# Moving a transpose, a masked product and a scaling between engines in the chunked delta-rule scan

## The chip, the cores and the metric

The kernel runs on one core of one Trainium2 chip. The metric is the device time of one execution in microseconds (us); the same program is executed several times and the median is reported. Engine names below are those of the profile: PE is TensorE (PEld its weight loads), DVE is VectorE, ACT is ScalarE, POOL is GpSimd, SP is SyncE, which issues the DMAs.

## The reference, cut to what matters

The model has two parts: a block with a gated delta-rule mixer and a feed-forward layer, and then two layers of a second network. The change lies in the delta-rule mixer alone. It works on chunks of 64 tokens, 8 heads, two directions, over 256 context tokens and 512 latent ones:

```
kk = k k^T                                   # per chunk, 64 x 64
a_mat = where(strict, beta * kk * decay, 0) + I
rhs = [v * beta, k * (beta * exp(gc))]
sol = triangular_solve(a_mat, rhs)           # unit lower triangle
u, w = sol[..., :dv], sol[..., dv:]
step:  v_new = u - w s
       o = (q * exp(gc)) s + (q k^T * decay) v_new
       s = s * exp(g_last) + k_dec^T v_new
```

All is float32.

## The kernel before

**The stages.** The program is written out per engine, in order, with semaphores between the engines; each engine executes its own list strictly in order. Two *scans*, one for each group of 4 heads (`hg` 0 and 1), stand between long projection stages. The functions `pe_scan`, `act_scan`, `dve_scan` and `pool_scan` hold the four engines' lists of a scan.

**Units and phases.** A scan has 12 units, `s` from 0 to 11. A unit is one chunk in each direction for 4 heads, with the two directions on the two halves of the 128 partitions. Units 0 to 3 are context, units 4 to 11 are latent. Each unit has five tiles of 128x512, shown as `u` in the profile: XY (X in columns 0 to 255, Y in 256 to 511), BA (A and, behind it, its transpose AT), EP, EQ and R. Tiles are shared by units that are 4 apart, which is why a unit's first phase waits until unit `s - 4` is done (`slot_free`).

The phases of a unit are

- `ga`: POOL makes the masked log decays in X.
- `kk`: PE multiplies k by k and sums the decays; ACT takes the exponential; POOL multiplies by beta; DVE makes A.
- `qk` (latent only): the decays for q and the product q k.
- `tr`: PE transposes A by 8 matmuls with the identity (`at`) and ACT copies the result into AT; POOL makes X = A * mask of level 0 (`x0`); DVE adds the identity to X (the *tr add*).
- `pt` (latent only): the transpose of the q k product.
- `ax` and `xy`, levels 1 to 5: the inverse of the triangular matrix is doubled level by level. `ax`: PE multiplies AT and X, DVE masks the product into E (the *level mask*). `xy`: PE multiplies E with X and Y, DVE adds both to XY. In `ax` of level 1 PE also makes Y as the transpose of X (`y0`, 8 matmuls with the identity) and ACT copies it into Y. In `ax` of levels 1 to 4, ACT makes one head of R = V * beta per level, in two halves (`bv`).
- `ks`: k times the state, and DVE adds it into R. `vn`: Y times R, the new values. `out`: PE makes the state's increment and the output; DVE updates the state tile `ss` with 8 instructions (the *state update*), then adds or ACT copies the output.

**The order.** `gdn_order()` interleaves the units in turns: in one turn each live unit has one phase, the oldest unit first. A unit joins every four or five turns, so that three or four are live. The same order holds on all four engines. In a turn with a `tr`, the unit in `tr` is the newest, and so its instructions stand last in the turn on each engine; the next instruction on DVE is then the first of the next turn, of an older unit. For latent units the turns around `tr` are

```
turn 36   5:vn   6:xy4  7:xy2  8:tr
turn 37   5:out  6:ax5  7:ax3  8:pt
turn 38   6:xy5  7:xy3  8:ax1  9:ga
...
turn 45   7:out  8:xy4  9:ax2  10:tr
turn 46   8:ax5  9:xy2  10:pt  11:ga
turn 47   8:xy5  9:ax3  10:ax1 11:kk
```

So on DVE the tr add is followed by the state update of the oldest unit (after units 4, 7, 8 and 11), or by an add or a level mask for PE (after 5, 6, 9 and 10). The context units have turns such as

```
turn 10   0:xy4  1:xy2  2:tr
turn 11   0:ax5  1:ax3  2:ax1
turn 12   0:xy5  1:xy3  2:xy1  3:ga
```

POOL's own list around these is `0tr 1ga 1kk 1tr 2ga 2kk 2tr 3ga 3kk 3tr 4ga 4kk 4qk 4tr 5ga ...`.

**PSUM.** All PE results go to a ring of 8 banks (`ps`), taken in order. Helper lines: L205 is any matmul, L224 any ACT activation, L236 a DVE or POOL tensor-tensor operation, L244 a DVE operation with a scalar and a tensor.

A matmul of float32 shows as two instructions in the trace, so that 8 matmuls are x16.

Of the kernel before, what the change touches and what calls it, by code (L numbers as in the profile page):

```python
# [66 lines left out]
def level_table():  # L67


    r, c = np.arange(128)[:, None], np.arange(64)[None, :]  # L70

    def mask(b, par):
        low = ((r % 64) // (2 * b) == c // (2 * b))
        low, up = low & ((r // b) % 2 == 1) & ((c // b) % 2 == 0), low & ((r // b) % 2 == 0) & ((c // b) % 2 == 1)
        return np.where(np.where((par + r // 64) % 2 == 0, low, up), -1.0, 0.0)

    out = [mask(b, par) for b in (1, 2, 4, 8, 16, 32) for par in range(2)]
    return np.concatenate(out, 1).astype(np.float32)


# [290 lines left out]
class Kernel:  # L371
# [56 lines left out]
    def layout(self):  # L428
# [32 lines left out]
        self.lbt = self.sb("lbt", m + 256, [128, 6, 16])  # L461
        self.sml = self.ring("sml", [self.sb("sml", m + 384 + 64 * i, [128, 64]) for i in range(8)])
        self.dec = self.ring("dec", [self.sb("dec", W + 33792 + 64 * i, [128, 64]) for i in range(4)])
        self.lvl = self.sb("lvl", B, [128, 12, 64])
        self.SS = self.sb("ss", B + 832, [128, 2, 512])
        self.bias = self.sb("bias", B, [128, 8, 384])

# [756 lines left out]
    def pe_scan(self, hg):  # L1224
# [6 lines left out]
        for s, ph in gdn_order():  # L1231
# [29 lines left out]
            elif ph == "pt":  # L1261
                b = K.ps.take(pe, "pt", *z)
                pe.wait_ge(dve.at("p", *z))
                for h in hs:
                    for r in rows:
                        pe.mm(Q(b, h)[r, :], Q(PP, h)[r, :], id_[r, r])
                pe.mark("pt", *z)
            elif ph[0] == "ax":
                lv = ph[1]
                b = K.ps.take(pe, "ax", *z, lv)  # L1270
                pe.wait_ge(act.at("at", *z), dve.at("xy", *z, lv - 1))
                for h in hs:
                    for r in rows:
                        pe.mm(Q(b, h)[r, :], Q(AT, h)[r, :], Q(X, h)[r, :])
                pe.mark("ax", *z, lv)
                if lv == 1:
                    b = K.ps.take(pe, "y0", *z)
                    for h in hs:
                        for r in rows:
                            pe.mm(Q(b, h)[r, :], Q(X, h)[r, :], id_[r, r])  # L1280
                    pe.mark("y0", *z)
            elif ph[0] == "xy":
                lv = ph[1]
                b = K.ps.take(pe, "xy", *z, lv)
                pe.wait_ge(dve.at("ev", *z, lv), act.at("y0", *z))
                for h in hs if lv < 5 else ():
                    for r in rows:
                        pe.mm(Q(b, h)[r, :], Q(Y, h)[r, :], Q(E, h)[r, :])
                for h in hs:
                    for r in rows:  # L1290
                        pe.mm(Q(b, 4 + h)[r, :], Q(E, h)[r, :], Q(Y, h)[r, :])
                pe.mark("xy", *z, lv)
            elif ph == "ks":
                b = K.ps.take(pe, "ks", *z)
                pe.wait_ge(dve.at("s", hg, s - 1))
                for h in hs:
                    for d, hf, c in pair:
                        pe.mm(H(b, h)[rows[hf], :], K.KT[:, h, tok[d]], H(K.SS[:, d, :], h))
                pe.mark("ks", *z)
            elif ph == "vn":  # L1300
                b = K.ps.take(pe, "vn", *z)
                pe.wait_ge(act.at("bv", *z) if s == 0 else dve.at("r", *z), dve.at("xy", *z, 5))
                for h in hs:
                    for r in rows:
                        pe.mm(H(b, h)[r, :], Q(Y, h)[r, :], H(R, h)[r, :])
                pe.mark("vn", *z)
                if lat:
                    b = [K.ps.take(pe, "o", *z, d) for d in range(2)]
                    pe.wait_ge(pool.at("q", *z))
                    for h in hs:  # L1310
                        for d, hf, c in pair:
                            pe.mm(Q(b[d], h), H(K.SS[:, d, :], h), EQ[:, h * 128 + hf * 64:h * 128 + hf * 64 + 64], h == 0, False,
                                  skip=True)
                    pe.mark("os", *z)
            elif ph == "out":
                if s < 11:
                    b = [K.ps.take(pe, "s", *z, d) for d in range(2)]
                    pe.wait_ge(dve.at("vd", *z))
                    for h in hs:
                        for d, hf, c in pair:  # L1320
# [17 lines left out]
    def act_scan(self, hg):  # L1338
# [3 lines left out]
        for s, ph in gdn_order():  # L1342
# [14 lines left out]
            elif ph == "pt":  # L1357
                act.wait_ge(pe.at("pt", *z))
                act.cp(EP[:, 256:512], K.ps[("pt", *z)][:, 0:256]).then_inc(act("pt", *z), 1)
                act.also("ps", "pt", *z)  # L1360
            elif ph[0] == "ax":
                h = ph[1] - 1
                if h == 0:
                    act.wait_ge(pe.at("y0", *z))
                    act.cp(XY[:, 256:512], K.ps[("y0", *z)][:, 0:256]).then_inc(act("y0", *z), 1)
                    act.also("ps", "y0", *z)
                for d, hf, c in K.pair(s) if h < 4 else ():
                    r = slice(64 * hf, 64 * hf + 64)
                    v, o = K.VM[r, c // 2, h * 128:h * 128 + 128], R[r, h * 128:h * 128 + 128]
                    act.a(o, v, ACT.Copy, scale=K.col(K.beta, s, hg, h)[r]).then_inc(act("bv", *z), 1)  # L1370
            elif ph == "vn":
                act.wait_ge(pe.at("vn", *z), dve.at("vd", *z) if s < 11 else None)
                act.cp(BA, K.ps[("vn", *z)]).then_inc(act("vn", *z), 1)
# [11 lines left out]
    def dve_scan(self, hg):  # L1385
# [5 lines left out]
        for s, ph in gdn_order():  # L1391
# [9 lines left out]
                dve.tt(PP, K.ps[("qk", *z)][:, 0:256], E, ALU.mult).then_inc(dve("p", *z), 1)  # L1401
                dve.also("ps", "qk", *z)
            elif ph == "tr":
                X = XY[:, 0:256]
                dve.wait_ge(pool.at("x0", *z))
                dve.tt(q4(X), q4(X), bc4(K.con("id64")), ALU.add).then_inc(dve("xy", *z, 0), 1)
            elif ph[0] == "ax":
                lv = ph[1]
                dve.wait_ge(pe.at("ax", *z, lv), dve.at("p" if lat else "a", *z) if lv == 1 else pe.at("xy", *z, lv - 1))
                b, m = K.ps[("ax", *z, lv)][:, 0:256], K.lvl[:, lv * 2 + par, :]  # L1410
                dve.tt(q4(E), q4(b), bc4(m), ALU.mult).then_inc(dve("ev", *z, lv), 1)
                dve.also("ps", "ax", *z, lv)
            elif ph[0] == "xy":
                lv = ph[1]
                w = slice(0 if lv < 5 else 256, 512)
                dve.wait_ge(pe.at("xy", *z, lv), dve.at("xy", *z, lv - 1), act.at("y0", *z))
                dve.tt(XY[:, w], XY[:, w], K.ps[("xy", *z, lv)][:, w], ALU.add).then_inc(dve("xy", *z, lv), 1)
                dve.also("ps", "xy", *z, lv)
            elif ph == "ks":
                dve.wait_ge(pe.at("ks", *z), act.at("bv", *z))  # L1420
                b = K.ps[("ks", *z)]
                for h in hs:
                    dve.stt(H(R, h), H(b, h), K.col(K.nbe, s, hg, h), ALU.mult, H(R, h), ALU.add).then_inc(dve("r", *z), 1)
# [25 lines left out]
    def pool_scan(self, hg):  # L1449
        K, pool, pe, act, dve = self, self.pool, self.pe, self.act, self.dve  # L1450
        pool.wait_ge(K.ended("chunks", hg), dve.at("nbe"))
        q4 = lambda ap: ap.rearrange("p (a b) -> p a b", b=64)
        v4 = lambda ap: ap.rearrange("p (a b) -> p a b", b=128)
        for s, ph in gdn_order():
            par, lat, (XY, BA, EP, EQ, R) = K.unit(s)
            z = (hg, s)
            X, A, E = XY[:, 0:256], BA[:, 0:256], EP[:, 0:256]
            if ph == "ga":
                pool.wait_ge(K.slot_free(z))
                pool.tt(q4(X), bc4(K.con(f"strict{par}")), bcl(K.cols(K.gg, s, hg), 64), ALU.mult).then_inc(pool("ga", *z), 1)  # L1460
            elif ph == "kk":
                pool.wait_ge(act.at("ev", *z))
                pool.tt(q4(A), q4(E), bcl(K.cols(K.beta, s, hg), 64), ALU.mult).then_inc(pool("eb", *z), 1)
                if lat:
                    pool.wait_ge(pool.at("eb", *z))
                    pool.tt(q4(E), q4(E), bc4(K.con(f"keep{par}")), ALU.mult).then_inc(pool("evm", *z), 1)
            elif ph == "qk":
                for d, hf, c in K.pair(s):
                    v = v4(EQ)[:, :, hf * 64:hf * 64 + 64]
                    pool.wait_ge(act.at("eq", *z))  # L1470
                    pool.tt(v, v, K.QT[:, :, (c - 4) * 64:(c - 3) * 64], ALU.mult).then_inc(pool("q", *z), 1)
            elif ph == "tr":
                pool.wait_ge(dve.at("a", *z), pe.at("kk", *z))
                pool.tt(q4(X), q4(A), bc4(K.lvl[:, par, :]), ALU.mult).then_inc(pool("x0", *z), 1)
            elif ph == "out":
                pool.mark("unit", *z)
        pool.mark("end", "scan", hg)
# [1685 lines left out]
```

## Time and profile before

| what | value |
|---|---|
| median of 3 executions | 4074.79 us (4074.69 to 4075.39) |
| profiled execution, its own time | 4075.39 us |
| its span in the profile | 4073.2 us |
| PE busy | 3790.8 us (93%) |
| DVE busy | 1935.7 us (48%) |
| ACT busy | 1510.6 us (37%) |
| POOL busy | 770.0 us (19%) |
| mean granted PE clock | 0.957 |

The span runs from the first to the last instruction of the profiled execution; the execution's own time is 2.2 us longer. "Busy" is the time in which an engine executed something; weight loads overlap the matmuls. The two scans lie at about 295 to 500 us and 640 to 851 us of the span, about a tenth of it.

### The profile page before, as it was taken

The numbers are of one execution on the slowest core, as the hardware profiler recorded it, in microseconds if no ns is written. First come the engines' busy times: TensorE is split into PE (matmuls) and PEld (weight loads), VectorE is DVE, ScalarE is ACT, GpSimd is POOL, SyncE is SP. The second block draws the span as 40 slices with busy tenths as digits, with TensorE's granted clock in tenths as the row PEclk, the third lists the DMA queues.
The fourth block names the chain that finished last, engine by engine and source line by source line (L and its number), as shares of the span: only waits on it lengthen the run. The fifth ranks groups of instructions, "written<-read, shape, count | busy, mean of one in ns | idle before, by whom it ended". The sixth has DMA issues, their size and how long they took to land.

```text
span 4073.2 us, 60895 instructions
## 1 busy us (share of the span) xinstructions
PE 3790.8 (93%) x25654; PEld 3075.0 (75%) x25654; DVE 1935.7 (48%) x3078; ACT 1510.6 (37%) x2533; POOL 770.0 (19%) x790
## 2 busy tenths in 40 slices
PE   6889998999999999988999999998999799999998
PEld 3568887887888747776888788875677688777886
DVE  5556555535444565635334533336465533444333
ACT  3433233323323345734223332224575422343222
POOL 0122122221211123432111110102244211101010
PEclk8999999989999899999999999998999899999999
DMA  5321010012222202111223122220111022222222
GB/s 183 125 84 18 3 52 13 3 53 104 99 96 96 68 16 72 59 58 37 97 95 119 59 97 99 97 79 26 62 63 63 16 96 96 88 102 84 98 94 87
DMA packets 81111, 300.87 MB, mean 74 GB/s; under 512 B 8776, under 2 KB 9928, under 8 KB 79944
## 3 DMA queue, kind: packets, MB, share of 16 engines
q1 hardware_dynamic: 80840, 296.99, 21.5%
q8 instruction: 203, 3.33, 0.3%
q14 instruction: 68, 0.56, 0.0%
HBM read 292.76 MB, written 4.19 MB: 73 GB/s over the span
## 4 chain that ended last, share of the span: by engine, by line
PE 75%; DVE 10%; ACT 6%; issue 5%; POOL 3%; DMA 1%; DVEq 0%; SPq 0%; POOLq 0%; ACTq 0%
PE ps L205 74%; PE ps L210 1%; DVE wlo L236 1%; DVE he L244 1%; ACT whi L224 1%; DVE hc L2334 1%; DVE tmp L244 1%; ACT ha L224 1%; DVE ac L244 1%; ACT wp L225 1%; DVE ha L236 1%; ACT L224 1%; DVE ss L244 1%; DVE q L236 1%; DMA wraw<-weights 0%
## 5 line engine op out<-in xcount | busy, mean ns | idle before, releaser
L236 DVE TENSOR_TENSOR wlo<-wraw,whi 128x1024 fp32r<-128x1024 f32 x537 | 682.1, 1275 | 771.6 <-ACT whi L224 770.9
L205 PE MATMUL ps<-hh,whi 128*128 128x512 f32 x1840 | 733.4, 399 | 19.1 <-DVE hl L236 13.9
L205 PE MATMUL ps<-hl,whi 128*128 128x512 f32 x1840 | 723.8, 393 | 0.0
L205 PE MATMUL ps<-hh,wlo 128*128 128x512 f32 x1840 | 723.5, 393 | 0.0
L224 ACT ACTIVATE whi<-wraw 128x1024 fp32r<-128x1024 f32 x537 | 559.8, 1050 | 223.1 <-PE ps L205 169.6
L205 PEld LDWEIGHTS ps<-hh,whi 128*128 128x128 f32 x1840 | 349.8, 190 | 103.7 <-ACT hh L224 20.1
L205 PEld LDWEIGHTS ps<-hh,wlo 128*128 128x128 f32 x1840 | 350.1, 190 | 74.7
L205 PEld LDWEIGHTS ps<-hl,whi 128*128 128x128 f32 x1840 | 350.7, 191 | 70.7
L205 PE MATMUL ps<-u,u 64*64 64x64 f32 (+2 forms) x6016 | 229.0, 228 | 25.6 <-DVE u L236 17.0
L205 PEld LDWEIGHTS ps<-u,u 64*64 64x64 f32 (+1 forms) x6016 | 209.5, 139 | 42.3 <-DVE u L236 18.1
L205 PE MATMUL ps<-gh,whi 128*128 128x512 f32 x528 | 205.4, 389 | 0.0
L205 PE MATMUL ps<-gl,whi 128*128 128x512 f32 x528 | 205.4, 389 | 0.0
L205 PE MATMUL ps<-gh,wlo 128*128 128x512 f32 x528 | 205.4, 389 | 0.0
L236 POOL TENSOR_TENSOR gl<-fv,gh 128x512 fp32r<-128x512 f32 x66 | 85.3, 1293 | 593.8 <-ACT gh L224 593.8
L236 POOL TENSOR_TENSOR sml<-sml,con 128x4 f32<-128x4 f32 (+3 forms) x36 | 60.5, 1681 | 665.7 <-DVE sml L241 603.6
L224 ACT ACTIVATE u<-ps 128x256 f32<-128x256 f32 (+1 forms) x128 | 57.7, 451 | 255.3 <-PE ps L205 189.4
L205 PE MATMUL ps<-fh,whi 128*128 128x512 f32 x352 | 138.5, 393 | 3.5 <-DVE fl L244 2.6
L205 PE MATMUL ps<-fl,whi 128*128 128x512 f32 x352 | 137.7, 391 | 0.0
L205 PE MATMUL ps<-fh,wlo 128*128 128x512 f32 x352 | 137.7, 391 | 0.0
L224 ACT ACTIVATE gh<-fv 128x512 fp32r<-128x512 f32 x66 | 41.7, 632 | 250.1 <-DVE fv L236 250.1
L236 DVE TENSOR_TENSOR x<-x,ps 128x512 f32<-128x512 f32 x64 | 44.0, 688 | 189.7 <-PE ps L205 189.7
L224 ACT ACTIVATE accs<-x 128x512 f32<-128x512 f32 x56 | 35.4, 632 | 243.6 <-DVE x L236 185.8
(391 smaller groups left out, 7145.7 us busy)
## 6 DMA issues: line engine op xcount, KB each, us to landing
wraw<-weights SPq DMA_DIRECT2D x537, 512.0 KB, 3.2
x<-xT SPq DMA_DIRECT2D x2, 2048.0 KB, 12.4
bias_lines<-ln SPq DMA_DIRECT2D x1, 2048.0 KB
xmf<-memT SPq DMA_DIRECT2D x2, 1024.0 KB, 4.7
out<-x SPq DMA_DIRECT2D x1, 2048.0 KB, 6.2
bias<-bias_lines SPq DMA_DIRECT2D x1, 1536.0 KB, 8.7
con<-consts SPq DMA_DIRECT2D x1, 1378.0 KB, 10.5
ctxt<-ctxT SPq DMA_DIRECT2D x1, 1024.0 KB, 12.5
```

The costliest lines, as they stand in the source:

```text
L205: self.last, self.open = self.e.matmul(out, lhsT, rhs, start=start, stop=stop, skip_group_check=skip), True
L210: self.last, self.open = self.e.transpose(out, in_, idn[0:k, 0:k]), True
L224: return self.e.activation(out, in_, func, bias=bias, scale=scale)
L225: return self.e.activation(out, in_, func, bias=bias, scale=scale, accum_out=acc)
L236: return self.e.tensor_tensor(out, a, b, op)
L244: return self.e.scalar_tensor_tensor(out=out, in0=a, scalar=s, in1=b, op0=op0, op1=op1)
L2334: dve.e.tensor_tensor_scan(C[:, r], rst[:, r], A[:, r], 0.0, ALU.mult, ALU.add).then_inc(dve("hb", *z), 1)
```

## The change

Four edits, all in the scan:

1. `y0` is gone: PE no longer transposes X, ACT no longer copies Y. Instead POOL's product in `tr` covers both halves of XY: X = A * mask and Y = AT * mask of the other direction. Its masks lie beside each other in the table `lvl`, which has 13 rows instead of 12. It now waits for ACT's copy of AT, beside the wait for A.
2. DVE's tr add covers 512 columns instead of 256.
3. `bv` moves from ACT (8 instructions of 64x128 per unit) to POOL (2 instructions of 64x512 per unit), in `ax` of level 2. POOL waits for its own last instruction before each, and for the end of each before it goes on (`halved`).
4. The consumers wait for the new producers: `vn` of unit 0 and `ks` wait for POOL's `bv`; `xy` no longer waits for `y0`.

```diff
@@ level_table
-    out = [mask(b, par) for b in (1, 2, 4, 8, 16, 32) for par in range(2)]
+    out = [mask(1, 0), mask(1, 1), mask(1, 0)] + [mask(b, par) for b in (2, 4, 8, 16, 32) for par in range(2)]
@@ pe_scan
                 pe.mark("ax", *z, lv)
-                if lv == 1:
-                    b = K.ps.take(pe, "y0", *z)
-                    for h in hs:
-                        for r in rows:
-                            pe.mm(Q(b, h)[r, :], Q(X, h)[r, :], id_[r, r])
-                    pe.mark("y0", *z)
...
-                pe.wait_ge(dve.at("ev", *z, lv), act.at("y0", *z))
+                pe.wait_ge(dve.at("ev", *z, lv))
...
-                pe.wait_ge(act.at("bv", *z) if s == 0 else dve.at("r", *z), dve.at("xy", *z, 5))
+                pe.wait_ge(pool.at("bv", *z) if s == 0 else dve.at("r", *z), dve.at("xy", *z, 5))
@@ act_scan
-            elif ph[0] == "ax":
-                h = ph[1] - 1
-                if h == 0:
-                    act.wait_ge(pe.at("y0", *z))
-                    act.cp(XY[:, 256:512], K.ps[("y0", *z)][:, 0:256]).then_inc(act("y0", *z), 1)
-                    act.also("ps", "y0", *z)
-                for d, hf, c in K.pair(s) if h < 4 else ():
-                    r = slice(64 * hf, 64 * hf + 64)
-                    v, o = K.VM[r, c // 2, h * 128:h * 128 + 128], R[r, h * 128:h * 128 + 128]
-                    act.a(o, v, ACT.Copy, scale=K.col(K.beta, s, hg, h)[r]).then_inc(act("bv", *z), 1)
@@ dve_scan
             elif ph == "tr":
-                X = XY[:, 0:256]
-                dve.wait_ge(pool.at("x0", *z))
-                dve.tt(q4(X), q4(X), bc4(K.con("id64")), ALU.add).then_inc(dve("xy", *z, 0), 1)
+                dve.wait_ge(pool.at("xy0", *z))
+                dve.tt(q4(XY), q4(XY), bc4(K.con("id64"), 8), ALU.add).then_inc(dve("xy", *z, 0), 1)
@@ pool_scan
             elif ph == "tr":
-                pool.wait_ge(dve.at("a", *z), pe.at("kk", *z))
-                pool.tt(q4(X), q4(A), bc4(K.lvl[:, par, :]), ALU.mult).then_inc(pool("x0", *z), 1)
+                pool.wait_ge(dve.at("a", *z), act.at("at", *z), pe.at("kk", *z))
+                m = K.lvl[:, par:par + 2, :].unsqueeze(2).broadcast_to([128, 2, 4, 64])
+                t = lambda ap: ap.rearrange("p (a h b) -> p a h b", a=2, h=4)
+                pool.tt(t(XY), t(BA), m, ALU.mult).then_inc(pool("xy0", *z), 1)
+                last = pool.at("xy0", *z)
+            elif ph == ("ax", 2):
+                for d, hf, c in K.pair(s):
+                    r = slice(64 * hf, 64 * hf + 64)
+                    pool.wait_ge(halved, pool.at("xy0", *z), K.slot_free(z), last)
+                    pool.tt(v4(R)[r], v4(K.VM[r, c // 2, :]), bcl(K.cols(K.beta, s, hg)[r], 128), ALU.mult).then_inc(pool("bv", *z, hf), 1)
+                    halved = pool.at("bv", *z, hf)
+                pool.also("bv", *z)
```

## Rows read from the trace of the kernel before

**Rows 1.** Busy time by engine in the two scans; columns as printed.

```profile
core 0: us, PE busy (x) PEld busy (x) DVE busy (x) ACT busy (x) POOL busy (x), PEclk, DMA share, GB/s
295.00:500.00 205.00, 188.47 (x4362) 172.22 (x4362) 116.55 (x295) 67.91 (x168) 39.29 (x60) 0.97 0.10 13
645.00:851.00 206.00, 192.64 (x4390) 176.83 (x4386) 116.11 (x294) 66.84 (x167) 37.84 (x58) 0.96 0.01 3
```

**Rows 2.** The chain that ended last, in order of time: start us, us, what.

```profile
377.41 0.04 issue
377.45 34.77 PE ps L205 x804
```

**Rows 3.** Who waited for whom, first scan: us in total, times, longest us.

```profile
DVE u L236 <- POOL u L236: 33.5, 14, 10.0
```

**Rows 4.** Groups of instructions, first scan: count, busy us, mean ns, idle before.

```profile
L224 ACT ACTIVATE u<-vm,beta 64x128 f32<-64x128 f32 x96 | 37.0, 396 | 1.8
L236 DVE TENSOR_TENSOR u<-u,ps 128x512 f32<-128x512 f32 x48 | 32.6, 686 | 21.3 <-PE ps L205 21.0
...
L205 PEld LDWEIGHTS ps<-con,u 64*64 64x64 f32 x512 | 18.5, 140 | 4.6 <-DVE u L236 4.6
...
L236 POOL TENSOR_TENSOR u<-u,lvl 128x256 f32<-128x256 f32 x12 | 8.7, 724 | 2.3 <-DVE u L236 2.3
```

**Rows 5.** Groups of POOL instructions, start of the span to 860 us.

```profile
L236 POOL TENSOR_TENSOR kt<-ac,sg 128x512 f32<-128x512 f32 x8 | 10.3, 1288 | 0.0
```

**Rows 6.** Timeline around `tr` of unit 8: start us, us, engine, instruction, idle before.

```profile
410.42 0.55 PEld L205 LDWEIGHTS ps<-con,u 64*64 64x64 f32 x16
...
411.16 0.39 ACT L224 ACTIVATE u<-ps 128x256 f32<-128x256 f32 x1 [3.02 <-PE ps L205]
411.30 0.42 DVE L236 TENSOR_TENSOR u<-u,con 128x256 f32<-128x256 f32 x1
...
412.25 2.16 DVE L244 SCALAR_TENSOR_TENSOR ss<-ss,ex,ps 128x128 f32<-128x128 f32 x8 [0.54 <-PE ps L205]
...
414.79 1.94 PEld L205 LDWEIGHTS ps<-u,u 64*64 64x64 f32 x64 [0.26 <-DVE u L236]
```

**Rows 7.** Timeline around `tr` of unit 2.

```profile
319.98 0.55 PEld L205 LDWEIGHTS ps<-con,u 64*64 64x64 f32 x16
...
320.52 0.61 POOL L236 TENSOR_TENSOR u<-con,gg 128x256 f32<-128x256 f32 x1
320.71 0.39 ACT L224 ACTIVATE u<-ps 128x256 f32<-128x256 f32 x1 [2.10 <-PE ps L205]
320.87 0.55 DVE L236 TENSOR_TENSOR u<-u,con 128x256 f32<-128x256 f32 x1
...
321.34 1.37 DVE L236 TENSOR_TENSOR u<-ps,lvl 128x256 f32<-128x256 f32 x3
...
322.46 4.25 PEld L205 LDWEIGHTS ps<-u,u 64*64 64x64 f32 x128
```

**Rows 8.** Timeline, the tr add of unit 0 beside a POOL instruction.

```profile
301.16 0.61 POOL L236 TENSOR_TENSOR u<-con,gg 128x256 f32<-128x256 f32 x1
301.24 0.82 DVE L236 TENSOR_TENSOR u<-u,con 128x256 f32<-128x256 f32 x1 [0.84 <-POOL u L236]
```

**Rows 9.** Timeline around `tr` of unit 10.

```profile
443.90 1.41 POOL L236 TENSOR_TENSOR u<-u,qt 128x256 f32<-128x256 f32 x2 [4.47 <-ACT u L224]
...
448.34 0.39 ACT L224 ACTIVATE u<-ps 128x256 f32<-128x256 f32 x1 [1.06 <-PE ps L205]
...
448.88 0.42 DVE L236 TENSOR_TENSOR u<-ps,lvl 128x256 f32<-128x256 f32 x1
...
450.01 1.55 PEld L205 LDWEIGHTS ps<-u,u 64*64 64x64 f32 x48
```

**Rows 10.** Timeline around `tr` of unit 6.

```profile
376.66 0.39 ACT L224 ACTIVATE u<-ps 128x256 f32<-128x256 f32 x1 [2.23 <-PE ps L205]
...
378.18 0.42 DVE L236 TENSOR_TENSOR u<-ps,lvl 128x256 f32<-128x256 f32 x1
...
379.31 1.55 PEld L205 LDWEIGHTS ps<-u,u 64*64 64x64 f32 x48
```

More of the change, by code:

```diff
@@ L463, in layout @@
         self.dec = self.ring("dec", [self.sb("dec", W + 33792 + 64 * i, [128, 64]) for i in range(4)])
-        self.lvl = self.sb("lvl", B, [128, 12, 64])
+        self.lvl = self.sb("lvl", B, [128, 13, 64])
         self.SS = self.sb("ss", B + 832, [128, 2, 512])
@@ L1409, in dve_scan @@
                 dve.wait_ge(pe.at("ax", *z, lv), dve.at("p" if lat else "a", *z) if lv == 1 else pe.at("xy", *z, lv - 1))
-                b, m = K.ps[("ax", *z, lv)][:, 0:256], K.lvl[:, lv * 2 + par, :]
+                b, m = K.ps[("ax", *z, lv)][:, 0:256], K.lvl[:, 1 + lv * 2 + par, :]
                 dve.tt(q4(E), q4(b), bc4(m), ALU.mult).then_inc(dve("ev", *z, lv), 1)
@@ L1415, in dve_scan @@
                 w = slice(0 if lv < 5 else 256, 512)
-                dve.wait_ge(pe.at("xy", *z, lv), dve.at("xy", *z, lv - 1), act.at("y0", *z))
+                dve.wait_ge(pe.at("xy", *z, lv), dve.at("xy", *z, lv - 1))
                 dve.tt(XY[:, w], XY[:, w], K.ps[("xy", *z, lv)][:, w], ALU.add).then_inc(dve("xy", *z, lv), 1)
@@ L1419, in dve_scan @@
             elif ph == "ks":
-                dve.wait_ge(pe.at("ks", *z), act.at("bv", *z))
+                dve.wait_ge(pe.at("ks", *z), pool.at("bv", *z))
                 b = K.ps[("ks", *z)]
@@ L1453, in pool_scan @@
         v4 = lambda ap: ap.rearrange("p (a b) -> p a b", b=128)
+        halved = None
         for s, ph in gdn_order():
@@ L1457, in pool_scan @@
             X, A, E = XY[:, 0:256], BA[:, 0:256], EP[:, 0:256]
+            pool.wait_ge(halved)
             if ph == "ga":
@@ L1460, in pool_scan @@
                 pool.tt(q4(X), bc4(K.con(f"strict{par}")), bcl(K.cols(K.gg, s, hg), 64), ALU.mult).then_inc(pool("ga", *z), 1)
+                last = pool.at("ga", *z)
             elif ph == "kk":
@@ L1463, in pool_scan @@
                 pool.tt(q4(A), q4(E), bcl(K.cols(K.beta, s, hg), 64), ALU.mult).then_inc(pool("eb", *z), 1)
+                last = pool.at("eb", *z)
                 if lat:
@@ L1466, in pool_scan @@
                     pool.tt(q4(E), q4(E), bc4(K.con(f"keep{par}")), ALU.mult).then_inc(pool("evm", *z), 1)
+                    last = pool.at("evm", *z)
             elif ph == "qk":
@@ L1471, in pool_scan @@
                     pool.tt(v, v, K.QT[:, :, (c - 4) * 64:(c - 3) * 64], ALU.mult).then_inc(pool("q", *z), 1)
+                    last = pool.at("q", *z)
             elif ph == "tr":
-                pool.wait_ge(dve.at("a", *z), pe.at("kk", *z))
-                pool.tt(q4(X), q4(A), bc4(K.lvl[:, par, :]), ALU.mult).then_inc(pool("x0", *z), 1)
+                pool.wait_ge(dve.at("a", *z), act.at("at", *z), pe.at("kk", *z))
[10 more added lines that the diff above has]
+                pool.also("bv", *z)
             elif ph == "out":
```

## The prediction

> **What bounds the kernel now.** I read the table of busy time by stretch first, because the change touches only the two scans, a tenth of the span. In the first scan PE is busy for 188.47 of 205.00 us, in the second for 192.64 of 206.00; DVE for 116, ACT for 67 and POOL for 38 to 39 [rows 1]. So PE is the bound of a scan and only some 13 to 17 us of idle PE time are left in each. The chain that ended last says the same in order of time: from 377.45 us it stays on PE for 34.77 us without a break [rows 2], and outside of such stretches it goes over DVE. Two consequences. Work taken from PE is worth its full length; work taken from ACT is worth nothing unless something waited for it. And DVE, busy for only 57%, does its work in order: PE waits as soon as one DVE instruction in its list is held up by more than the lead that PE has. What holds DVE up before is mostly POOL: 33.5 us in 14 waits [rows 3], which are the waits in `kk`, that the change leaves alone, and the start. The second scan has the same list on every engine; I work one out and take it twice.
>
> **The parts.**
>
> *PE without `y0`.* The `at`, `pt` and `y0` transposes are 32 blocks of 16 instructions in a scan; their weight loads, which set the pace, take 18.5 us for 512 [rows 4], so 0.58 us a block. 12 blocks go per scan: 12 x 0.58 = 7.0 us. This is the gain, 13.9 us in both scans if PE loses nothing in return.
>
> *ACT without the copy of Y and without `bv`.* 96 instructions of 396 ns and 12 of 0.39 [rows 4, 6] are 42 us of ACT per scan. But ACT waited for PE before each of the AT copies that I looked at (2.10, 2.23, 3.02 and 1.06 us idle) [rows 6, 7, 9, 10]. No queue stood in front of them, so nothing starts sooner. I count nothing. If the cover were gone, a copy behind one `bv` piece would be 0.4 us late; the idle times exclude that here.
>
> *The product on POOL: later and longer.* Before, it needs only A and is finished before DVE comes to the tr add. Now it needs AT, and so stands behind PE's `at` and ACT's copy. Its length goes from 724 ns at 256 columns [rows 4] to what 512 columns of the same operation take: 1288 ns [rows 5]. Bounds from rows: 0.72, if the second half were free, and 1.45, if it were twice the first. The row has the same width and type, so I take 1.29. A hand-over between engines costs 0.04 us, as in the chain [rows 2].
>
> *The tr add* goes from 0.42 [rows 6] to 0.69, as the other 128x512 adds [rows 4].
>
> These two lie on one path: `at`, AT copy, product, tr add, and behind the tr add everything that stands later in DVE's list. How much reaches PE differs by unit.
>
> *Units 4, 7, 8, 11 (state update next).* Unit 8: the copy ends at 411.16 + 0.39 = 411.55, the product runs from 411.59 to 412.88, the add from 412.92 to 413.61. The state update, which began at 412.25, begins 1.35 us later. Behind it stand the level masks for which PE was already idle at 414.79 (0.26 us) [rows 6]. There is no lead left, so all 1.35 us reach PE. Four units: 5.4 us.
>
> *Units 5, 6, 9, 10 (an add or a level mask next).* Unit 10: copy ends at 448.73, product until 450.06, add until 450.79. The level mask moves from 448.88 to 450.75 and ends at 451.2. PE wants its result in the block that began at 450.01 [rows 9], so PE waits for 1.2 us, and a little more for the add behind: 1.3. Unit 6: copy ends at 377.05, product until 378.38, add until 379.11, mask from 379.1 to 379.5 instead of from 378.18; PE wanted it at 379.31 [rows 10]: 0.2 to 0.3. By the same sum unit 5 is like 6 and unit 9 a little under 10. I take 0.3, 0.3, 1.0 and 1.3: 2.9 us. The ends are 0 and the full delay of the mask, 0.9 to 1.9 each.
>
> *Units 0 to 3 (context).* There is no turn between `tr` and `ax` of level 1, so PE also waits directly for X. Unit 2: the copy ends at 321.10, the product at 322.43. POOL then goes on at once to `ga` of the next unit, 0.61 us, and this meets the tr add. The trace has that meeting: the add, 0.42 us when alone, took 0.82 and ended 0.29 us after the POOL instruction (301.77, 302.06), and took 0.55 and ended again 0.29 after it (321.13, 321.42) [rows 7, 8]. So the new add, 0.27 longer, ends 0.56 after `ga`: 322.43 + 0.02 + 0.61 + 0.56 = 323.62, instead of 321.42. `ax` level 1 of unit 2 (at least 0.48, a third of the 48-instruction block) follows at 323.66, and the next block, which began at 322.46 after `y0`, begins near 324.15: 1.7 us later, with the gain of `y0` already in it. Units 0 and 1 stand in the same order (`0tr 1ga`, `1tr 2ga`): 1.7 each. Behind unit 3, POOL waits elsewhere and DVE was busier: 1.0. Sum: 6.1 us.
>
> The Trainium skill ("SBUF — State Buffer", section "Who interferes with whom") has this as a rule: a VectorE instruction with two SBUF inputs contends with a GpSimd instruction that reads SBUF, and the later one to issue blocks until the first ends. By the full wait of the rule the add of unit 0 would have ended 0.4 after POOL, by the row 0.29; that is 0.1 us in three units per scan.
>
> *`bv` on POOL.* No POOL instruction of the trace has 64 partitions. Bounds: 0.64 us, half of 128x512, and 1.29, the whole. I take 1.2, two per unit, so 29 us more of POOL per scan: 39 becomes about 75 of 205 us with the longer products. Where could it be late? Before the product of unit 10, the tightest place: q's two products end at 445.31, then `bv` of unit 9 until 447.8, and the product is not ready before 448.77 [rows 9]. There is room for 1.7 us a piece. What is queued behind it on POOL (`kk`, `qk` of the next unit) waits for ACT for longer than that. R is wanted only in `ks`, ten turns on. So `bv` costs nothing in the sum.
>
> The Trainium skill ("GPSIMD Engine Reference", section "2. Architecture") gives each of the 8 cores 16 fixed partitions. By that rule 64 partitions would take as long as 128, 1.29 us; no row here shows it, and the sum would be the same.
>
> *DMA, tables and banks.* The level table is one row longer, in one load at the start. The ring loses a bank user per unit, which can only free banks sooner.
>
> **The sum** per scan: 6.1 + 5.4 + 2.9 - 8 x 0.58 = 9.8 us. Two scans: 19.5 us. On the profiled execution's own 4075.4 us (span 4073.2) this is 4094.9; that execution was 0.6 over the median, so I say 4094.5.
>
> **The rivals.**
>
> *The stalls hide and `y0` decides (faster).* PE has a lead over DVE, the stalls eat only that, and 13.9 us remain as gain: 4061. It decides if PE's lead at the tr add is over 1.35 us in every latent unit and the context units cost no more than `y0`. Units 5 and 6 come near. Against it: the idle PE time before 414.79, and the context units, where PE itself needs X. Chance 0.10.
>
> *Only the context units show (no change).* The latent stalls are hidden but those of units 0 to 3 not: 2 x 6.1 - 2 x 8 x 0.58 = +2.9, so 4078; with half of the state-update stalls, +8.3, the border. Chance 0.15.
>
> *The tr add is also kept out by `bv` (slower still).* After units 0, 1 and 2 POOL's list has `ga` and then both `bv` pieces with nothing to wait for but POOL itself. If POOL takes up the next piece before the blocked add gets in, each of these 6 adds loses another 1.2 to 2.4 us: +7 to +14, so 4102 to 4109. For it: the add did get in only after the POOL instruction's end in rows 7 and 8. Against: POOL waits for its own completion in between, which leaves a gap. Chance 0.15. In the same direction, full exposure in the four mask units adds 2 x 3 = 6 us.
>
> The Trainium skill's rule of the exclusive lock, named above, is what would make this one bite.
>
> *The forecast*, a net loss of 12 to 27 us: 0.60.
>
> **How the numbers follow.** A measurement of this kernel tells 0.2%, 8 us, from no change. Slower by more: the forecast 0.60 and the lock rival 0.15: 0.75. Within 0.2%: 0.15. Faster: 0.10. The forecast's own range is 4087 to 4102. The low end of the range goes into the no-change case, 4080, the high end to the end of the lock rival with a product of 1.45 us, 4111. What is left out is the faster case and half of the no-change case.
>
> **What would show it.** In the profile after: POOL's product at about 1.29 us, beginning 0.04 to 0.1 after ACT's copy; in the list of waits, DVE waiting for POOL about 12 times more per scan and some 15 to 20 us more in total; PE waiting for DVE by about 15 us more; PE busy 7 us less per scan, and each scan 9 to 10 us longer. The state update after `tr` of unit 8 should begin more than 2 us after PE's `at` ends, and not 1.2. ACT should be near 25 us busy. If scans are longer but DVE's waits are not, my mechanism is wrong; if DVE waits and PE does not, PE's lead was larger than I read. The prediction fails if POOL needs much less than 1.29 us for 512 columns, or if the turn has slack that a single unit's rows don't show: a late DVE instruction that lets PE run on with the next phase, and catches up.

## The result and the profile after

| | time |
|---|---|
| before, 6 executions beside the changed kernel | 4079.11 us median (4074.69 to 4094.03) |
| changed kernel, 6 executions | 4113.70 us median (4109.05 to 4118.91) |
| ratio | 1.0082, 95% interval 1.0062 to 1.0100 |
| profiled execution of the changed kernel | 4119.53 us, span 4117.7 us |

The change makes the kernel slower by 33 us (25 to 41). The forecast was slower, but by 19.5 us, and its 4094.5 and its range (4080 to 4111) end below the measured median. About 4 us of the distance is the kernel before itself, whose first three executions, on which the forecast stood, were at its low end; the rest is the change.

I measure a scan from the start of the first A on DVE to the start of the last level mask. In the first profiles the second scan goes from 195.9 to 213.5 us, +17.6; +9.8 was forecast. Two windows that each run from about that first A to just behind the last mask split this into idle and busy time of PE. Columns as in [rows 1]; the kernel before:

```profile
644.00:842.00 198.00, 185.16 (x4338) 170.20 (x4340) 115.41 (x291) 66.24 (x166) 38.11 (x58) 0.98 0.01 3
```

and the changed kernel:

```profile
673.00:888.00 215.00, 186.62 (x4140) 170.24 (x4142) 120.31 (x291) 25.86 (x58) 70.82 (x82) 0.94 0.01 3
```

PE idles for 215.00 - 186.62 = 28.4 us instead of 12.8: +15.6. And it is busy for 1.5 us *more*, although 192 instructions (the 12 blocks of `y0`) are gone, which were worth 7.0 us. The granted clock over the window went from 0.98 to 0.94.

Around `tr` of unit 8, second scan, the changed kernel's timeline answers to [rows 6]:

```profile
797.10 0.55 PEld L205 LDWEIGHTS ps<-con,u 64*64 64x64 f32 x16
...
797.83 0.38 ACT L224 ACTIVATE u<-ps 128x256 f32<-128x256 f32 x1 [3.03 <-PE ps L205]
798.35 1.26 POOL L236 TENSOR_TENSOR u<-u,lvl 128x512 f32<-128x512 f32 x1 [4.25 <-DVE u L236]
...
799.64 0.69 DVE L236 TENSOR_TENSOR u<-u,con 128x512 f32<-128x512 f32 x1 [1.59 <-POOL u L236]
...
800.25 2.15 DVE L244 SCALAR_TENSOR_TENSOR ss<-ss,ex,ps 128x128 f32<-128x128 f32 x8
...
802.79 1.94 PEld L205 LDWEIGHTS ps<-u,u 64*64 64x64 f32 x64 [1.58 <-DVE u L236]
```

Read it downwards: transposes, copy, product, add, state update, and then PE, each waiting for the one above. The state update begins 3.15 us after the start of `at` instead of 1.83 [rows 6]: 1.32 late, 1.35 was forecast. PE's wait goes from 0.26 to 1.58 us. The waits of the second scan (us in total, times, longest) say the same, after:

```profile
DVE u L236 <- POOL u L236: 51.0, 24, 10.0
...
PE ps L205 <- DVE u L236: 27.4, 20, 3.2
```

and before:

```profile
DVE u L236 <- POOL u L236: 33.5, 14, 10.0
...
PE ps L205 <- DVE u L236: 12.2, 12, 3.2
```

DVE has ten more waits for POOL, 17.5 us in total, and PE waits 15.2 us more for DVE.

Stretches of 10 us at the start of the second scan show where the clock went. The changed kernel:

```profile
668.00:678.00 10.00, 3.73 (x43) 2.74 (x45) 1.51 (x2) 2.05 (x3) 3.98 (x5) 0.50 0.01 2
678.00:688.00 10.00, 8.40 (x143) 6.96 (x140) 2.55 (x5) 0.72 (x2) 1.93 (x3) 0.60 0.01 2
688.00:698.00 10.00, 7.25 (x210) 6.54 (x208) 4.81 (x9) 0.43 (x2) 4.78 (x5) 1.00 0.01 2
698.00:708.00 10.00, 7.99 (x196) 7.76 (x193) 5.72 (x12) 0.57 (x2) 4.17 (x4) 0.83 0.02 4
708.00:718.00 10.00, 8.10 (x199) 7.37 (x199) 5.79 (x12) 1.18 (x3) 2.45 (x3) 0.93 0.01 2
718.00:728.00 10.00, 10.00 (x215) 9.11 (x213) 5.17 (x12) 1.58 (x3) 4.73 (x6) 0.90 0.01 3
728.00:738.00 10.00, 7.63 (x168) 7.24 (x166) 5.77 (x16) 0.77 (x2) 1.88 (x2) 0.83 0.01 2
```

The kernel before, in its first profile:

```profile
640.00:650.00 10.00, 5.62 (x77) 4.47 (x75) 1.67 (x3) 3.52 (x7) 1.91 (x3) 0.50 0.00 0
650.00:660.00 10.00, 8.19 (x219) 7.30 (x217) 4.40 (x9) 3.76 (x11) 1.91 (x3) 0.97 0.01 3
660.00:670.00 10.00, 9.75 (x287) 9.14 (x286) 6.24 (x13) 3.40 (x10) 1.92 (x3) 1.00 0.02 4
```

and in another one, `before_again`:

```profile
655.00:665.00 10.00, 7.50 (x113) 6.76 (x114) 2.78 (x5) 2.25 (x6) 1.30 (x2) 0.50 0.01 2
665.00:675.00 10.00, 9.75 (x214) 8.31 (x215) 4.68 (x9) 4.13 (x11) 1.91 (x3) 0.81 0.01 3
675.00:685.00 10.00, 10.00 (x292) 9.53 (x294) 6.40 (x13) 4.04 (x11) 1.91 (x3) 1.00 0.02 4
```

All these scans begin at half clock (0.50, the level of 1.2 GHz); before them PE had little to do (2.29 us busy between 630 and 640 us in the first profile of the kernel before). When the clock comes up is no mark of the change: 6.4 us after the first A in the first profile of the kernel before, 13.7 and 14.0 in its two others, 13.1 and 13.2 in the two of the changed kernel. What the change brings is that the clock falls back behind waits. In the changed kernel's profile above it does so three times, for 10 us in all: the stretches at 0.83, at 0.93 and 0.90 (one fall across their border), and at 0.83. Each began within 1.5 us of the end of a wait of 1.9 to 2.4 us, those behind `tr` of units 2, 3 and 4. In its second profile, `after_again`, the same three waits were followed by one fall. In no second scan of the kernel before does the clock fall back. A block of 64 instructions that follows a wait of 2.37 us shows what such a fall means:

```profile
733.79 3.43 PEld L205 LDWEIGHTS ps<-u,u 64*64 64x64 f32 x64 [2.51 <-DVE u L236]
733.79 3.57 PE L205 MATMUL ps<-u,u 64*64 64x64 f32 x64 [2.37 <-DVE u L236]
```

Its weight loads take 3.43 us, where those of the same block at full clock take 1.94, before the change [rows 6] as behind `tr` of unit 8 after it. The Trainium skill ("TensorE: Matmul & The Clock Gate", "Part 1: The HAM clock gate") says that the clock has two levels and is set by how busy PE was of late. By that rule a wait can cost more than its own length, and this block agrees, with 1.5 us on top of its wait.

### The profile page after: what moved, and what is told of

It reads as the page before. It is cut to its first block, busy times and chain, and to the rows that moved or that the text cites. A ratio compares the mean times of both kernels' runs of the same rounds, so it can differ in the third digit from the quotient of the medians.

```text
span 4117.7 us, 59944 instructions
## 1 busy us (share of the span) xinstructions
PE 3797.1 (92%) x25270; PEld 3078.3 (75%) x25270; DVE 1945.4 (47%) x3078; ACT 1429.2 (35%) x2317; POOL 834.5 (20%) x838
## 4 chain that ended last, share of the span: by engine, by line
PE 64%; DVE 9%; ACT 5%; issue 3%; POOL 2%; DVEq 0%; POOLq 0%; ACTq 0%
PE ps L205 63%; DVE he L244 1%; PE ps L210 1%; DVE wlo L236 1%; DVE hc L2333 1%; ACT ha L224 1%; ACT wp L225 1%; DVE ha L236 1%; DVE tmp L244 1%; DVE q L236 1%; ACT whi L224 0%; ACT L224 0%; DVE ws L244 0%; POOL u L236 0%; DVE hl L236 0%
## 5 line engine op out<-in xcount | busy, mean ns | idle before, releaser
L205 PE MATMUL ps<-u,u 64*64 64x64 f32 (+2 forms) x6016 | 241.2, 236 | 62.5 <-DVE u L236 47.6
L205 PEld LDWEIGHTS ps<-u,u 64*64 64x64 f32 (+1 forms) x6016 | 220.8, 146 | 81.8 <-DVE u L236 33.2
L205 PE MATMUL ps<-gh,whi 128*128 128x512 f32 x528 | 205.4, 389 | 0.0
L205 PE MATMUL ps<-gl,whi 128*128 128x512 f32 x528 | 205.4, 389 | 0.0
L205 PE MATMUL ps<-gh,wlo 128*128 128x512 f32 x528 | 205.4, 389 | 0.0
L224 ACT ACTIVATE u<-ps 128x256 f32<-128x256 f32 (+1 forms) x104 | 48.4, 466 | 382.0 <-PE ps L205 289.1
L236 POOL TENSOR_TENSOR mg<-mg,mg 128x512 f32<-128x512 f32 x32 | 54.5, 1702 | 324.5 <-DVE mg L236 324.5
## 6 DMA issues: line engine op xcount, KB each, us to landing
ctxt<-ctxT SPq DMA_DIRECT2D x1, 1024.0 KB, 11.6
```

What stands on the lines that cost most here:

```text
L205: self.last, self.open = self.e.matmul(out, lhsT, rhs, start=start, stop=stop, skip_group_check=skip), True
L224: return self.e.activation(out, in_, func, bias=bias, scale=scale)
L236: return self.e.tensor_tensor(out, a, b, op)
```

## The experiments

Lengths of the scans in the profiles, from the first A to the last level mask, and the whole kernel by its ratio to the kernel before (us worked out with 4080):

| kernel | first scan | second scan | ratio (95% interval) | us |
|---|---|---|---|---|
| before (three profiles) | 195.8, 207.8, 208.4 | 195.9, 197.4, 197.4 | 1 | 0 |
| changed (two profiles) | 219.7, 219.5 | 213.5, 210.3 | 1.0082 (1.0062 to 1.0100) | +33 |
| `y0_only` | 218.5 | 213.6 | 1.0071 (1.0051 to 1.0092) | +29 |
| `bv_pool` | 196.8 | 196.8 | 0.9986 (0.9969 to 1.0003) | -6 |
| `wait_only` | 216.7 | 205.4 | 1.0039 (1.0025 to 1.0054) | +16 |
| `fill` | 224.5 | 207.2 | 1.0053 (1.0035 to 1.0070) | +22 |
| `fill_before` | 214.7 | 201.0 | 1.0022 (1.0006 to 1.0038) | +9 |
| `late_add` | 210.3 | 205.3 | 1.0008 (0.9994 to 1.0021) | +3 |
| `late_fill` | 213.8 | 197.9 | 0.9999 (0.9985 to 1.0013) | 0 |
| `split_ctx` | 213.2 | 204.3 | 1.0023 (1.0009 to 1.0037) | +9 |
| `split` (two profiles) | 191.7, 205.1 | 192.1, 192.1 | 0.9948 (0.9929 to 0.9968) | -21 |
| `split_bvact` | 199.5 | 191.8 | 0.9959 (0.9943 to 0.9974) | -17 |
| `lines_late` | 212.4 | 215.1 | 1.0097 (1.0080 to 1.0114) | +40 |

**Which part costs.** `y0_only` is the changed kernel with `bv` back on ACT.

```diff
@@ act_scan, against the changed kernel
+            elif ph[0] == "ax":
+                h = ph[1] - 1
+                for d, hf, c in K.pair(s) if h < 4 else ():
...
+                    act.a(o, v, ACT.Copy, scale=K.col(K.beta, s, hg, h)[r]).then_inc(act("bv", *z), 1)
```

> The changed kernel with bv left on ACT, as before the change: y0 is gone, the product and the tr add are wide and late. Theory A (late tr add, and through it TensorE's granted clock at the start of each scan): the whole loss is here, each scan 16 to 19 us longer than before, total +30 to +38 us. Theory B (bv on POOL keeps the tr add out or makes POOL late): most of the loss is gone, total within 10 us of before.

`bv_pool` is the other half alone: the kernel before with `bv` as two POOL pieces in `ax` of level 2, as in the change's diff.

> The kernel before with bv alone moved to POOL (2 pieces per unit in ax of level 2). Theory A: no change, within 5 us of before; the scans keep their 196 us from the end of the first A to the last level mask. Theory B: +15 to +35 us, and DVE waits for POOL longer than 34 us per scan.

The loss is in `y0_only` (213.6 us, +29) and none in `bv_pool` (196.8 us, -6). So it is not POOL's added work in `bv`. In the changed kernel's first scan, with the same columns as [rows 4], a `bv` piece takes 1089 ns:

```profile
L236 POOL TENSOR_TENSOR u<-vm,beta 64x512 f32<-64x512 f32 x24 | 26.1, 1089 | 2.1
...
L236 POOL TENSOR_TENSOR u<-u,lvl 128x512 f32<-128x512 f32 x12 | 15.2, 1265 | 25.4 <-DVE u L236 18.6 <-ACT u L224 2.8 <-issue 2.4
```

**The wait alone.** `wait_only` is the kernel before with one wait added; product and add stay narrow and `y0` stays.

```diff
-                pool.wait_ge(dve.at("a", *z), pe.at("kk", *z))
+                pool.wait_ge(dve.at("a", *z), act.at("at", *z), pe.at("kk", *z))
```

> The kernel before, with nothing changed but that POOL's x0 product (still 256 columns) also waits for ACT's copy of AT. y0 and its copy stay. Theory A: the product starts as late as in the changed kernel but is 0.54 us shorter and the add 0.27 shorter, while the 7 us of y0 per scan are not gained: each scan +12 to +18 us, total +24 to +36. Theory C (the length of the wide product is what costs, not the wait): total under +10 us.

The second scan grows by 8 to 9.5 us and the kernel by 16 (10 to 22), under the 12 to 18 per scan and the 24 to 36 in total that I expected. The narrow product and add make the path 0.8 us shorter (0.54 and 0.27), and some of the waits are gone: behind `tr` of units 5, 6 and 7 PE has no new one. But the wait costs without any wide instruction, so theory C, which put the whole loss on their length, falls. It does not do all of it: from the first A to the last mask PE idles for 19.2 us here, 28.5 in the changed kernel and 11.5 in the later profiles of the kernel before. About half of the added idle time comes with the wait alone, the rest with the longer product and add behind it. The granted clock of this scan is 0.97, with no fall in it.

**The clock.** `fill` gives PE useless work where it stands idle.

```diff
@@ pe_scan, tr
                 pe.mark("at", *z)
+                if s < 4:
+                    b = K.ps.take(pe, "fl", *z)
+                    for _ in range(8):
+                        pe.mm(b[:, 0:128], id_, id_)
+                    pe.mark("fl", *z)
```

> The changed kernel with useless work added: after the at transposes of each context unit (8 units in both scans) PE does 8 matmuls of 128x128 float32 with the identity into a spare bank, nearly 2 us each time, where it stood idle for 1.9 to 3.1 us. Its output is not used. Theory A: TensorE's granted clock stays at 2.4 GHz from the first units on (0.9 or more in the stretches where the changed kernel shows 0.60 to 0.93), and the scans get 5 to 8 us shorter each despite the added work. Theory D (only the stalls count, the clock is a by-product): the scans stay as long or get up to 4 us longer each.

The second scan falls from 213.5 (210.3 in the other profile) to 207.2 us with more work in it, 3 to 6 us where 5 to 8 were expected. The granted clock is at 0.95 in the second stretch and does not fall back:

```profile
672.00:682.00 10.00, 6.82 (x52) 5.64 (x50) 1.51 (x2) 2.05 (x3) 3.96 (x5) 0.50 0.00 0
682.00:692.00 10.00, 8.08 (x160) 6.96 (x160) 3.04 (x6) 0.77 (x2) 3.43 (x4) 0.95 0.01 2
692.00:702.00 10.00, 9.25 (x234) 8.47 (x229) 5.11 (x10) 0.77 (x2) 3.96 (x5) 1.00 0.01 3
702.00:712.00 10.00, 9.97 (x260) 9.15 (x260) 6.47 (x13) 0.98 (x2) 3.83 (x5) 1.00 0.02 4
712.00:722.00 10.00, 9.96 (x236) 9.03 (x234) 5.92 (x11) 0.77 (x2) 2.70 (x4) 1.00 0.01 3
722.00:732.00 10.00, 8.36 (x208) 7.77 (x203) 6.73 (x20) 1.96 (x4) 5.13 (x6) 1.00 0.01 3
```

The control is the same filling in the kernel before.

> A control: the kernel before with the same useless matmuls (8 of 128x128 after the at of each context unit). Here PE has little idle time at these places and its clock is already up from the second unit on. Theory A: the filling is no help here, it costs most of its own length, up to 1.9 us in each of the 4 units, less what the first unit wins by an earlier clock: a scan takes 197 to 203 us, total 0 to +14. If it shortens the scan by over 2 us, the gain seen in the changed kernel is not the removal of the change's own clock loss.

There it costs: 201.0 us instead of 196 to 197. The filling has two effects, and the control parts them. It brings the clock up earlier in both kernels, 6.6 us after the first A in `fill` and 3.8 in `fill_before`, where it mostly takes 13 to 14; this is not the change's own loss. And in `fill` alone it stands in idle time that the change made, and the falls of the clock behind the waits of units 2, 3 and 4 are gone. So `fill` shows that idle time and clock hang together; how much of its 3 to 6 us each effect brings it does not show.

**Which units.** `late_add` lets DVE do the tr add of latent units one phase later.

```diff
@@ dve_scan, against the changed kernel
-            elif ph == "tr":
+            elif ph == ("pt" if lat else "tr"):
```

> The changed kernel with one thing moved: for latent units DVE does the tr add one phase later, in pt, so that nothing of an older unit is queued behind its wait in the tr turn. Theory A (what costs is DVE's in-order wait for the late product): the idle PE time of 1.4 to 2.4 us after the tr of units 4, 8, 9, 10 and 11 goes away, the gain of y0 in the latent units stays, and a scan takes 198 to 204 us from the first A to the last level mask instead of 213.5; the loss in the first three context units stays. Total +5 to +18 us on the kernel before. Theory C (the length of product and add costs, wherever the add stands): a scan stays over 209 us.

The second scan is 205.3 us. I expected 198 to 204. Idle time did what theory A says: over the window from the first A to just behind the last mask it is

```profile
652.50:859.20 206.70, 186.78 (x4136) 170.77 (x4136) 118.77 (x290) 25.87 (x58) 70.34 (x82) 0.94 0.01 3
```

206.70 - 186.78 = 19.9 us, 8.5 less than in the changed kernel; the forecast had 5.4 + 2.9 = 8.3 for the latent stalls. But PE is as busy as in the changed kernel (186.78 for 186.62) and the clock is still 0.94. The total, +3 us, is below the +5 to +18 expected. With the filling of the context units on top:

> The late add of latent units and the filling of PE in context units together (8 useless matmuls of 128x128 after the at of each context unit; their output is not used). Theory A: the late add took 8.2 us off a scan (213.5 to 205.3), the filling 6.2 (213.5 to 207.2), and the two act on different units, so a scan takes 198 to 200 us; what is then left over the 191 us of a scan with no stall at all is the stall of the context units alone. Total within 8 us of the late add less 12. If the two overlap, a scan stays over 202 us.

197.9 us: the clock is back (0.99 over the window) and the kernel is level with the one before. The converse repairs the context units alone (X and Y as in `split` below for `s < 4`, wide and late for the rest):

```diff
@@ dve_scan, against the changed kernel
+                if s < 4:
+                    dve.wait_ge(pool.at("x0", *z))
+                    dve.tt(q4(XY[:, 0:256]), q4(XY[:, 0:256]), bc4(K.con("id64")), ALU.add).then_inc(dve("xy", *z, 0), 1)
+                else:
...
```

> The changed kernel with the parted product and adds for context units alone; latent units keep the late wide product and the wide tr add. Theory A: the context units' stalls and the clock loss go, 13 us of a scan (late add 205.3 against parted 192.1), the latent stalls of 8 us stay: a scan takes 199 to 202 us, total +5 to +12 us on the kernel before. If the clock loss comes from the latent units' stalls as well, the scan stays over 204 us.

204.3 us, over the 199 to 202 expected. My idea that the clock is lost in the context units alone falls: with them repaired the clock still falls back just behind PE's wait of 2.41 us behind `tr` of unit 4, and that stretch is at 0.83.

```profile
710.00:720.00 10.00, 9.30 (x198) 8.54 (x200) 5.38 (x15) 0.39 (x1) 1.87 (x3) 0.83 0.01 2
```

**A version without the stall.** `split` keeps what was good (no `y0`) and undoes the late tr add: X is made at once, Y in a second product, and its identity is added behind the level mask of level 1, one phase before PE needs it.

```diff
@@ pool_scan, tr, against the changed kernel
-                pool.wait_ge(dve.at("a", *z), act.at("at", *z), pe.at("kk", *z))
...
-                pool.tt(t(XY), t(BA), m, ALU.mult).then_inc(pool("xy0", *z), 1)
+                pool.wait_ge(dve.at("a", *z), pe.at("kk", *z))
+                pool.tt(q4(X), q4(A), bc4(K.lvl[:, par, :]), ALU.mult).then_inc(pool("x0", *z), 1)
+                pool.wait_ge(act.at("at", *z))
+                pool.tt(q4(XY[:, 256:512]), q4(BA[:, 256:512]), bc4(K.lvl[:, par + 1, :]), ALU.mult).then_inc(pool("xy0", *z), 1)
@@ dve_scan, tr and ax
-                dve.wait_ge(pool.at("xy0", *z))
-                dve.tt(q4(XY), q4(XY), bc4(K.con("id64"), 8), ALU.add).then_inc(dve("xy", *z, 0), 1)
+                dve.wait_ge(pool.at("x0", *z))
+                dve.tt(q4(XY[:, 0:256]), q4(XY[:, 0:256]), bc4(K.con("id64")), ALU.add).then_inc(dve("xy", *z, 0), 1)
...
+                if lv == 1:
+                    Y = XY[:, 256:512]
+                    dve.wait_ge(pool.at("xy0", *z))
+                    dve.tt(q4(Y), q4(Y), bc4(K.con("id64")), ALU.add).then_inc(dve("yi", *z), 1)
```

> The changed kernel with the two halves parted again: POOL makes X from A at once (256 columns, no wait for AT), DVE adds the identity to X in tr as before the change; POOL makes Y from AT in a second product, and DVE adds the identity to Y (256 columns) in ax of level 1, behind the level mask. y0 stays gone, bv stays on POOL. Theory A: no stall after tr is left, the clock rises as early as in the kernel before (0.96 or more from the second unit on), and a scan is the 196 us of before less up to 7 us of y0: 188 to 193 us, total -6 to -16 us on the kernel before, a gain. Theory B or C (POOL's longer work or the clock by itself): scans of 196 us or more.

> As split, with bv back on ACT. Theory A: the same time as split within 3 us, since neither engine is a bound. If POOL's bv matters beside the second product, this one is faster than split by 4 us or more.

Both beat both kernels: 0.9948 and 0.9959, that is 21 us (13 to 29) and 17 us (11 to 23) less than before, with a second scan of 192 us. In `split`'s window PE idles as little as in the kernel before:

```profile
644.00:837.50 193.50, 181.47 (x4141) 166.06 (x4142) 119.57 (x303) 25.87 (x58) 72.42 (x94) 0.96 0.01 3
```

193.50 - 181.47 = 12.0 us idle, and 3.7 us less busy than in the first profile of the kernel before. That profile had the early clock, though. Compared at equal clock (0.96, and up 13 to 14 us after the first A), from the first A to the end of the last mask, PE is busy for 186.3 us in `before_again`, `before_third` and `bv_pool` and for 180.3 to 180.5 in the three profiles of `split` and `split_bvact`: 5.8 us less. That is what `y0` is worth once nothing takes it back. The -21 us of `split` go beyond the -6 to -16 expected. Where `bv` runs makes no difference that the intervals can tell.

**The first scan.** In the changed kernel it was 6 us longer than the second, and PE stood still there without a semaphore to wait for:

```profile
341.11 2.17 PE L205 MATMUL ps<-u,u 64*64 64x64 f32 x36 [4.76 <-issue]
```

`lines_late` moves the 2 MB write of the bias lines, which overlaps this part, to the projections between the scans.

```diff
-            if b == K.block_of["c", 0, "v", 3] + NRAW:
+            if b == K.block_of["c", 1, "q", 1] + NRAW:
                 K.load("lines", K.line, ...)
```

> The changed kernel with the 2 MB write of the bias lines, which runs over the first 35 to 40 us of the first scan, moved to the projections between the scans. In the profiles of all slower kernels so far PE stood 4 to 13 us in the first scan, waiting for no semaphore, until about when this write ended. Theory E (PE waits for its instructions, which are fetched behind that write): the stall is gone, the first scan is as long as the second (213 us), and the time falls by 4 to 8 us against the changed kernel. If the stall stays or turns up elsewhere in the scan, the write is not its cause.

There is no standstill in the first scan (212.4 us), but one profile says little, since three of the other kernels' 16 have none either. The kernel is no faster (+40 us); in its projections there is now a wait of 7.9 us that the changed kernel does not have:

```profile
590.57 0.76 PE L205 MATMUL ps<-hhi,whi 128*128 128x512 f32 x1 [7.90 <-DVE wlo L236]
```

The expected 4 to 8 us did not come. Four more profiles are of kernels already shown:

> The kernel before, unchanged, for another profile. In 9 of 12 profiles PE stood 4 to 13 us in the first scan for no semaphore, but not in that of the kernel before. Theory F (the stall comes and goes with the execution and has nothing to do with the change): it shows in about two of three profiles of any kernel, so in this one or in its sister with a chance near 0.9; the first scan is then 203 to 212 us and the second stays at 196. If neither shows it, it belongs to kernels whose first units are late.

> As the other look at the kernel before: by theory F a stall of 4 us or more in the first scan with a chance of about two in three, the second scan 196 us in any case.

> The changed kernel, unchanged, for another profile. The second scan takes 213 to 214 us again, with the granted clock between 0.6 and 0.93 in most of its second to seventh stretches of 10 us; the first scan 213 us plus whatever PE stands still in it for no semaphore, from 0 to 13 us by theory F.

> The parted version, unchanged, for another profile. Second scan 192 us again. First scan 192 us, or by theory F 196 to 205 with a stall of 4 us or more; its first profile had none.

The kernel before has it too, 8.54 us in one and 8.77 in the other; here the latter:

```profile
327.58 0.91 PE L205 MATMUL ps<-con,u 64*64 64x64 f32 x12 [8.77 <-issue]
```

and the parted version, which had none in its first profile, now 11.66. In all, 13 of the 16 profiles with the write in its place show it, with 4.1 to 13.3 us. Theory F stands: it belongs to the execution, not to the change. Its end is not tied to the write's end. In nine of the 13 the two lie within 3 us, but in `before_again`, `before_third`, `late_add` and `split_ctx` PE goes on 8 to 10 us before the write is done. What the end does follow, in all 13, is a packet of 16 KB on the instruction queue (q8 in the DMA view): PE goes on 2.2 to 2.5 us after it starts. In `before_third` this queue moves nothing from 283 us until the packet that starts at 325.1, and PE goes on at 327.6; between 324 and 328 us:

```profile
q8 instruction: 1, 0.02, 1.4%
```

The first profile of the kernel before, without a standstill, has between 283 and 325 us:

```profile
q8 instruction: 4, 0.07, 0.7%
```

## Why the prediction was wrong

**Right.** PE is the bound, DVE's in-order wait in `tr` is where the change hurts, and its size: the stalls forecast per scan are 6.1 + 5.4 + 2.9 = 14.4, and with the `y0` already taken off in the four context units (about 0.5 each) 16.4 us of PE idle time. Measured: +15.6 in the first profiles, +16.8 between the second ones (28.4 against 11.6 us idle). Unit by unit, second scan, the new waits of PE are 2.5, 2.0, 2.0 and 1.9 us behind `tr` of units 0 to 3, 5.0 us in units 4, 7, 8 and 11 (forecast 5.4), and 0, 0.6, 1.2 and 1.5 in units 5, 6, 9 and 10 (0.3, 0.3, 1.0 and 1.3). The delay of the state update (1.32 for 1.35), the product (1265 ns for 1.29 us), `bv` (1089 ns, nobody waits), ACT at nothing (25.86 us busy and no gain) and the clash of the tr add with `ga` (the add takes 1.08 us and ends 0.54 after `ga`, for 0.56) came as worked out. Small misses: POOL took up the product 0.14 us after ACT's copy, not 0.04, which was read from an "issue" row of PE's chain and from no hand-over; and the add clashes with `ga` in units 3, 5, 6, 9 and 10 as well, where the forecast had none.

**The step that failed** is "PE without `y0`": "12 x 0.58 = 7.0 us. This is the gain", and with it the sum, which set 8 x 0.58 against the stalls. PE's busy time did not fall by 7.0 us; it rose by 1.5 in the first pair of profiles and fell by 4.0 in the second pair (187.28 to 183.25). Over the four second scans with the wide late add (`after`, `after_again`, `y0_only`, `lines_late`) and the four without it (the three of the kernel before and `bv_pool`) it is 185.4 against 185.6 us on average, from the first A to the end of the last mask: PE idles 16.5 us more, as forecast, and is busy 0.2 us less instead of 7.0.

The runs show what stood in its place. The term itself is worth 5.8 us, not 7.0 (`split`). The other 5.5 us were given back because PE's other work ran slower: the sum had no term for the granted clock. By the granted clock in the traces, the four scans with the late add are at half clock for 23, 17, 27 and 28 us, the four without it for 6, 14, 14 and 14. What is new is the falls of the clock behind the waits, 10, 3, 14 and 14 us against none. By my estimate, half their length, they cost 5 us on average. In `split`, which has no `y0` and no late add, there are no falls and the gain is there. How many falls an execution has varies: in the second pair of profiles there is one, and the clock takes less than 2 us. Part of the first pair's difference is also no effect of the change, since that profile of the kernel before had the early clock.

The lengths follow: the four second scans with the late add (213.5, 210.3, 213.6, 215.1) stand at 213.1 on average, the four without it (195.9, 197.4, 197.4, 196.8) at 196.9. That is 16.2 us per scan where I had 9.8, and twice that is the 33 us measured.

**The second, smaller miss** is the base. The forecast was built on three executions of 4074.7 to 4075.4 us and a profile without the standstill in the first scan; later medians of the kernel before were 4084 to 4087 us.

**The rivals.** That the stalls hide failed in every unit but 5; unit 6 shows 0.6 us. That the tr add is kept out by `bv` did not happen: in units 0 to 2 it ended as computed with `ga` alone, while POOL had already begun the first `bv` piece, and `y0_only` without any `bv` on POOL is as slow.

**Open.** The whole-kernel gain of `split` (-21 us) and the small loss of `late_add` (+3) are each 11 to 14 us better than twice their second scan would make them (-10 and +17). The difference lies outside the scans or in the first one, where executions of one kernel differ by as much; I can't say whether it belongs to these versions.

## What to carry to other kernels

When an operation in an in-order list gets one more producer to wait for, don't price it by its own slack: look at who stands behind it in that list and serves the bounding engine. If two halves of a result become ready at different times, keep them two instructions, and put the late one where its consumer is, not where it is made. And price the idle time of TensorE above its length: waits of 1.9 to 3.1 us in a row cost here about a third as much again on average (5.5 on 16.5 us), through the clock, and in one profile only about a tenth.

## What was not expected of the hardware

Useless matmuls in TensorE's gaps shortened a scan by 3 to 6 us. The granted clock over the scan was 0.94 to 0.96 without them and 0.98 with them. And TensorE stood still for 4 to 13 us for no semaphore in 13 of 16 profiles; each standstill began in the first scan while a 2 MB write was under way on the DMA queues. Each of the 13 standstills ended 2.2 to 2.5 us after a 16 KB packet on the instruction queue had started. That TensorE waits there for its instructions is argued from this timing, which holds 13 times out of 13. That the write is what makes the packet late is not shown: the same write ran beside three scans without a standstill, and there is only one profile with the write elsewhere.
